# Attention probabilities transposed on VectorE in 32x32 blocks, and head sums and the sample's attention on small TensorE tiles

## The reference

```python
q, k, v, b_gate, c_gate, h, g_attn, g_conv = split(rmsnorm(x) @ w_in)
q, k = rope(rmsnorm_per_head(q)), rope(rmsnorm_per_head(k))
# prompt: chunk c sees chunks c-2, c-1 and c; sample: 128 cached keys and its own 32
s = (q @ k.T) * SCALE                      # masked to NEG_INF outside the window
m = max(max(s), sink)
p = exp(s - m) / (sum(exp(s - m)) + exp(sink - m))
attn = p @ v
u = c_gate * h;  conv_y = conv3(u)
merged = sigmoid(g_attn) * (attn @ w_attn_proj) + sigmoid(g_conv) * ((b_gate * conv_y) @ w_conv_proj)
x = x + merged @ w_out
y = x + (silu(xn @ w_ffn_gate) * (xn @ w_ffn_up)) @ w_ffn_down      # xn = rmsnorm(x)
```

## Time and profile before

| | us |
|---|---|
| median of 3 runs | 1734.26 |
| lowest and highest | 1733.05, 1735.46 |
| the profiled execution, its own time | 1733.39 |
| its span in the trace | 1731.6 |

### The profile page before, as it was taken

How to read it: one execution, slowest core, us unless ns; L and a number is a source line. 1 busy time by engine, 2 the same in 40 slices (tenths; PEclk the granted TensorE clock), 3 DMA queues, 4 the chain that set the end, 5 groups by cost and what they waited for, 6 DMA issues and landing times.

```text
span 1731.6 us, 35651 instructions
## 1 busy us (share of the span) xinstructions
PE 1714.1 (99%) x13944; PEld 1699.0 (98%) x13944; DVE 1014.1 (59%) x1268; ACT 809.4 (47%) x985; POOL 31.5 (2%) x54
## 2 busy tenths in 40 slices
PE   8899999999999999999999999999999999999999
PEld 7899999999999999999999999999999999999999
DVE  7876776767754444555565655554455554455565
ACT  6445655455554444434444555543344443334443
POOL 0100000000000000000000000000000000000000
PEclk9899999999999999999999999999999999999999
DMA  7455455555566566556566555565556556556555
GB/s 241 152 159 158 145 157 158 162 153 158 157 213 185 178 181 179 176 175 186 160 194 193 164 177 182 170 192 175 179 171 186 176 175 187 175 177 183 174 176 153
DMA packets 298626, 302.73 MB, mean 175 GB/s; under 512 B 9488, under 2 KB 296336, under 8 KB 298464
## 3 DMA queue, kind: packets, MB, share of 16 engines
q1 hardware_dynamic: 296544, 296.00, 56.4%
q0 software_dynamic: 752, 3.80, 0.6%
q10 hardware_dynamic: 1296, 2.46, 0.5%
HBM read 299.50 MB, written 2.72 MB: 175 GB/s over the span
## 4 chain that ended last, share of the span: by engine, by line
PE 97%; DVE 1%; DMA 1%; issue 0%; ACT 0%; SPq 0%; DVEq 0%; ACTq 0%
PE acc L1007 31%; PE acc L1009 31%; PE acc L1008 31%; DMA raw<-in_w_in 1%; PE side L1104 1%; PE side L1128 0%; PE side L1116 0%; PE side L1092 0%; DVE w_lo L595 0%; DMA region_x<-in_x_t 0%; PE side L1106 0%; DVE region_m L661 0%; PE side L1118 0%; PE side L1131 0%; ACT w_hi L373 0%
## 5 line engine op out<-in xcount | busy, mean ns | idle before, releaser
L595 DVE TENSOR_TENSOR w_lo<-raw,w_hi 128x1024 fp32r<-128x1024 f32 x567 | 688.6, 1225 | 537.0 <-ACT w_hi L373 528.8
L373 ACT ACTIVATE w_hi<-raw 128x1024 fp32r<-128x1024 f32 x567 | 593.2, 1054 | 612.9 <-PE acc L1009 608.4
L1007 PE MATMUL acc<-xn_hi,w_hi 128*128 128x288 f32 x2976 | 855.2, 287 | 1.1 <-DVE w_lo L595 1.1
L1008 PE MATMUL acc<-xn_lo,w_hi 128*128 128x288 f32 x2976 | 851.9, 286 | 0.0
L1009 PE MATMUL acc<-xn_hi,w_lo 128*128 128x288 f32 x2976 | 851.9, 286 | 0.0
L1007 PEld LDWEIGHTS acc<-xn_hi,w_hi 128*128 128x128 f32 x2976 | 563.3, 189 | 2.5 <-issue 1.5
L1008 PEld LDWEIGHTS acc<-xn_lo,w_hi 128*128 128x128 f32 x2976 | 563.3, 189 | 0.1
L1009 PEld LDWEIGHTS acc<-xn_hi,w_lo 128*128 128x128 f32 x2976 | 563.2, 189 | 0.0
L1007 PE MATMUL acc<-at_hi,w_hi 128*128 128x288 f32 x1216 | 347.9, 286 | 0.5 <-DVE w_lo L595 0.5
L1008 PE MATMUL acc<-at_lo,w_hi 128*128 128x288 f32 x1216 | 347.8, 286 | 0.0
L1009 PE MATMUL acc<-at_hi,w_lo 128*128 128x288 f32 x1216 | 347.8, 286 | 0.0
(11 more groups left out here) (180 smaller groups left out, 755.1 us busy)
## 6 DMA issues: line engine op xcount, KB each, us to landing
raw<-in_w_in SPq DMA_DIRECT2D x199, 512.0 KB, 4.4
raw<-in_w_ffn_gate SPq DMA_DIRECT2D x88, 512.0 KB, 4.5
raw<-in_w_ffn_up SPq DMA_DIRECT2D x88, 512.0 KB, 4.4
raw<-in_w_ffn_down SPq DMA_DIRECT2D x64, 512.0 KB, 3.7
raw<-in_w_attn_proj SPq DMA_DIRECT2D x32, 512.0 KB, 4.5
raw<-in_w_conv_proj SPq DMA_DIRECT2D x32, 512.0 KB, 4.4
raw<-in_w_out SPq DMA_DIRECT2D x32, 512.0 KB, 4.6
raw<-in_w_ffn_down SPq DMA_DIRECT2D x32, 384.0 KB, 3.7
```

The lines of the kernel that those rows point to most:

```text
L373: nc.scalar.activation(w_hi[:, s], raw[:, s], ACT.Copy).then_inc(S["hi_ready"], 1)
L595: V.tensor_tensor(w_lo[:, s], raw[:, s], w_hi[:, s].bitcast(F32), ALU.subtract).then_inc(S["lo_ready"], 1)
L1007: te.matmul(out, w_hi[:, s, k, cols], hi_b, start=first, stop=False)
L1008: te.matmul(out, w_hi[:, s, k, cols], lo_b, start=False, stop=False)
```

## The change

- VectorE transposes the probabilities with its own 32x32 block transposition (`STREAM_TRANSPOSE`, L758 and L834 of the changed kernel) from `probs` straight to their places in a new SBUF tile `probs_t`. There are sixteen of them per round over a 32-partition strip each; blocks that the mask makes zero in all heads are left out (`probs_t` is zeroed once at the start). They run in three parts, `turn_probs(0)` to `turn_probs(2)`, between the pieces of group g+3. The fourteen transposes on TensorE and the four copies on ScalarE are gone, and with them the semaphores `probs_normed`, `probs_in_psum` and `probs_copied`; `heads_out` waits for `probs_turned` and `values_staged`.
- The sums of squares are made by 64x64 tiles, one for each half of the rows and of the frames: 16 + 4 products in place of 4 + 1. The scores of the sample are two 64-row products in place of one of 128 rows, and its exponential, maximum and normalization are done in two halves of 64 partitions. `stats` has ten columns in place of nine.
- The sample's probabilities are transposed within 32x32 blocks by one instruction, and its output is made of 20 products of 32 rows, 64 columns and 32 frames each, in place of 4. Its values are laid out for that by 20 small copies on GpSimd, once in two rounds.
- VectorE does piece (g+3, 3) and (g+4, 0) ahead of the convolution taps in place of behind them; ScalarE does `at_hi` ahead of `z_hi`.

```diff
+            by_block = [a.rearrange("p u (m k) -> p u m k", m=3) for a in (probs, probs_t[:])]
+            def turn_probs(part):
+                for q in range(4):
+                    for r in range(4):
+                        middle_only, no_middle = q < 2 and r > 1, q > 1 and r < 2
+                        groups = slice(1, 2) if middle_only else slice(0, 3, 2) if no_middle else slice(0, 3)
+                        if (q * 4 + r) % 3 != part:
+                            continue
+                        of, to = (t[32 * p:32 * p + 32, :, groups, 32 * k:32 * k + 32]
+                                  for t, p, k in ((by_block[0], q, r), (by_block[1], r, q)))
+                        last = V.transpose(to, of)
+                if part == 2:
+                    last.then_inc(S["probs_turned"], 1)
...
-                V.tensor_scalar(probs_sample, probs_sample, s_inv[:, 8:9], None, ALU.mult
-                                ).then_inc(S["probs_normed"], 1)
+                for half in range(2):
+                    r = slice(64 * half, 64 * half + 64)
+                    own.mark(V.tensor_scalar(probs_sample[r], probs_sample[r], of_sample(s_inv, half), None, ALU.mult))
+                own.settle()
+                own.mark(V.transpose(probs_t_sample, probs_sample))
+                turn_probs(0)
                 ahead(g + 3, 1)
+                turn_probs(1)
                 ahead(g + 3, 2)
...
+                ahead(g + 3, 3)
+                turn_probs(2)
+                ahead(g + 4, 0)
                 for w in range(3):
...
-                ahead(g + 3, 3)
-
-                ahead(g + 4, 0)
                 ahead(g + 4, 1)
                 ahead(g + 4, 2)
...
             def head_sums(j):
-                pe.wait_ge(S["q_squared"], j + 2)
-                each_head = same_head.rearrange("p (h c) -> p h c", h=2)[:, :, 0]
+                wait_apart(pe, S["q_squared"], j + 2)
                 for n in range(2):
                     for t in range(2):
-                        c = 4 * n + 2 * t
-                        te.matmul(head_ssq[:, c:c + 2], head_b[:, t, n * HALF:n * HALF + P], each_head, start=True,
-                                  stop=True)
-                te.matmul(head_ssq[:, 8:9], squares_sample[:].rearrange("p h t n -> p (h t n)"), ones[:, 0:1],
-                          start=True, stop=True)
+                        for part in halves:
+                            for half, r in enumerate(halves):
+                                at = n * HALF + part.start
+                                te.matmul(head_ssq[part, half, 2 * n + t:2 * n + t + 1], head_b[r, t, at:at + 64],
+                                          ones[r, 0:1], start=True, stop=True)
+                for part in halves:
+                    for half, r in enumerate(halves):
+                        te.matmul(head_ssq[part, half, 4:5], squares_sample[r].rearrange("p t n -> p (t n)"),
+                                  ones[r, 0:1], start=True, stop=True)
...
-                for half, r in enumerate(rows):
-                    te.matmul(side[r, 1, 0:2 * TS], values_cur[:, 2], probs_t_sample[:, 0, r], start=True, stop=False)
-                for half, r in enumerate(rows):
-                    last = te.matmul(side[r, 1, 0:2 * TS], values_cur[0:TS, 3], probs_t_sample[0:TS, 1, r], start=False,
-                                     stop=True)
+                for kb in range(SAMPLE_BLOCKS):
+                    for q in range(4):
+                        half, t = q // 2, q % 2
+                        rows = slice(QUARTER * q, QUARTER * q + QUARTER)
+                        last = te.matmul(out_sample_t[halves[half], t], values_sample[rows, kb],
+                                         probs_t_sample[rows, kb * QUARTER:(kb + 1) * QUARTER], start=kb == 0,
+                                         stop=kb == SAMPLE_BLOCKS - 1)
```

More of the change, by code:

```diff
@@ L443, in _ @@
                 nc.scalar.activation(prompt(head_b), sums(0, slice(0, TP)), ACT.Square)
-                for half in range(2):
-                    r = slice(64 * half, 64 * half + 64)
-                    last = nc.scalar.activation(split(squares_sample[r, half]), sums(0, slice(TP, T))[r], ACT.Square)
-                last.then_inc(S["q_squared"], 1)
+                nc.scalar.activation(split(squares_sample), sums(0, slice(TP, T)), ACT.Square).then_inc(S["q_squared"], 1)
                 ahead(g + 2, 0)
@@ L744, in _ @@
                 own.settle()
-                for half in range(2):
-                    r = slice(64 * half, 64 * half + 64)
-                    last = V.tensor_copy(split(q_sample[r, half]), sample(head_a[r]))
-                last.then_inc(S["q_roped"], 1)
+                V.tensor_copy(split(q_sample), sample(head_a)).then_inc(S["q_roped"], 1)
                 dve.wait_ge(S["q_squared"], j + 2)
@@ L762, in _ @@
                             scalar=lowest, op0=ALU.add, op1=ALU.max, accum_out=s_max[:, c:c + 1]))
-                own.mark(V.reduce_max(s_max[:, 8:9], scores_sample, AX_X))
+                for half in range(2):
+                    own.mark(V.reduce_max(of_sample(s_max, half), scores_sample(half), AX_X))
                 dve.wait_ge(S["head_rms_ready"], j + 1)
@@ new lines, in all_scores @@
+                last.then_inc(S["scores_ready"], 1)
+            def heads_out(j):
+                pe.wait_ge(S["values_staged"], j + 1)
+                pe.wait_ge(S["probs_turned"], j + 1)
+                of_heads = probs_t[:].rearrange("p (t r) k -> p r t k", t=2)
+                for half, r in enumerate(halves):
+                    te.matmul(side[r, 0, :], values_cur[:, 0], of_heads[:, half, :, 0:2 * P], start=True, stop=False)
+                for half, r in enumerate(halves):
+                    te.matmul(out_t[r, :, P:2 * P], values_cur[:, 1], of_heads[:, half, :, 2 * P:3 * P], start=False,
+                              stop=True)
+                for kb in range(SAMPLE_BLOCKS):
+                    for q in range(4):
+                        half, t = q // 2, q % 2
[3 more added lines that the diff above has]
+                                         stop=kb == SAMPLE_BLOCKS - 1)
@@ L1150, in mix @@
                     if s == 1:
[L1152 removed]
+                        wait_apart(pe, S["side_free"], j + 1)
                         head_sums(j)
```

137 lines of the change are left out of this document (67 added, 70 removed).

## The result

The changed kernel takes 1744.54 us (median; 1744.13 to 1745.09), the kernel before, run beside it, 1733.92 us: 1.0062 times as long, 95% interval 1.005 to 1.0075, so 10.6 us more. I had predicted 1748, within 1729 to 1763, and slower with a chance of 0.72. Sign and size hold, but by luck: of the four terms only the first is right, the second has the wrong sign, the third is three times what it was, and the fourth, the one that decides, is a third of what it was. The errors cancel.

The account below looks back on a forecast made before the run. TensorE, busy 99% of the span, was taken to bound the kernel. Terms of -1.54 + 0.75 + 1.7 + 0.85 gave +1.76 us a round, +14.1 in 8 rounds: 1748 us median, range 1729 to 1763.

Parts of the forecast that it names:

- Term 1: The transposes on TensorE go, which takes 1.54 us a round off its path.
- Term 2: Head sums on TensorE by small tiles, 40 passes in place of ten: +0.75 us a round.
- the feed of 0.065 us a pass: Rate at which TensorE can be fed small passes, a load with its matmul: 40 passes take 2.6 us.
- rival A: Small passes on TensorE are fed fast enough and the change gains: -0.74 us a round, 1728 us; chance 0.17.
- Term 3: The sample's output on TensorE by small tiles, 20 products in 40 passes: +1.7 us a round.
- turn of the loop: Register work and branch behind the round's last pass on TensorE, no longer covered by lined-up passes: 0.5 us.
- Term 4: VectorE, with transpositions and other work added, comes late to piece (g+3, 1) and TensorE waits: +0.85 us a round.
- slack of 2.4 us: Time before the change between VectorE's `w_lo` for piece (g+3, 1), ready at 303.2, and TensorE beginning it at 305.63.
- The margin at (g, 3): Piece (g, 3), wanted 8.8 us into the next round, is ready at about 7 thanks to term 3's longer tail.
- Rival B: Transposing float32 on VectorE costs double: +5.1 us a round, 1775 us; chance 0.09.
- Rival C: Everything added is hidden and TensorE's losses equal its gains, feed about 0.04 us a pass: 1734 us; chance 0.12.
- the worse ends of terms 2 and 3: Upper ends for head sums, +1.7, and the sample's output, +2.8; together the round's sum was put at about +3.3 us.

Follow-up runs that it names:

- e9_no_turns_4of20: e1_no_turns with only 4 of the 20 small products of the sample's output (result wrong); 1719.04 us, 0.9916 of the kernel before.
- e11_sample_first: e10_rotated with the sample's 20 small products ahead of the four large ones at the end of the round; 1723.20 us, 0.9939 of the kernel before.
- e1_no_turns: The changed kernel without VectorE's sixteen transpositions of the prompt's probabilities (result wrong; the sample's stays); 1724.34 us, 0.9943 of the kernel before.
- e10_rotated: The changed kernel with VectorE's work reordered, ScalarE's first four exponentials one piece earlier, and piece (g, 3) prepared in the round before; 1724.49 us.
- e4_sample_4of20: The changed kernel with only 4 of the 20 small products of the sample's output (result wrong); 1743.97 us, 1.0055 of the kernel before.
- e5_exps_sooner: The changed kernel with VectorE's work reordered, ScalarE's first four exponentials ahead of piece (g+2, 2), and (g+2, 3) behind the last exponential; 1733.04 us.

## Why the prediction was right, and where not

- **Term 1, the transposes leave TensorE, -1.54 us a round: held** as far as it can be seen. TensorE's own round fell by 1.14; the other changes of its stream are read from rows, -0.41 (head sums), +0.15 (the sample's scores, 0.27 to 0.42) and +0.57 (`heads_out`, 1.81 to 2.38), which leaves -1.45 for the transposes.
- **Term 2, head sums, forecast +0.75, measured -0.41.** The step that failed is the feed of 0.065 us a pass, taken from a start after a wait. Those two rows are starts of an empty engine; the long row gives 0.015 us a pass. The scores start 0.69 us behind the head sums, by my own check a sign for rival A. The lower of my two prices, 0.055 us for a step of four tiles side by side, gave a gain of 0.3 and was nearly right. The Trainium skill, page "TensorE: Matmul & The Clock Gate", gives in section "Wait — 56ns, not 53.3ns?" about 62 ns per matmul with hardware decode off; at the 15 ns a pass measured here, that price is not the one paid. The same page of the Trainium skill, section "Part 3: Packing small matmuls — row/col tiling", has matmuls in different tiles start about 4 ns apart; the 15 ns agree with it in that small passes overlap, not in the figure.
- **Term 3, the sample's output, forecast +1.7, measured +0.57.** Same step, same cause; e9_no_turns_4of20 measures 32 of the 40 passes on their own, 0.69 us with the uncovered turn of the loop. The sentence on the turn of the loop was right in kind, since it is uncovered now, but it is 0.16 us and not 0.5. e11_sample_first covers it again.
- **Term 4, VectorE late, forecast +0.85, measured 2.54** (54.97 less 52.43). The place, the mechanism and the slack of 2.4 us were right. The size was wrong in three pieces. The first transpositions with the sample's take 2.92 us (308.11 to 311.03) and not 2.2, because each has about 0.18 us beyond its elements (2.66 us for six of 1536 elements at 1.02 ns) and not 0.07. The second exponential costs 0.68 (303.85 to 305.00 are 1.15 for two, where one took 0.47), not 0.47, the second half of the normalization 0.45 with its waits (2.86 in place of 2.41), not 0.31. Together 4.05 in place of 3.0, against a slack of 2.4 and the 0.15 by which the sample's longer scores hold TensorE back: 1.5, near the 1.45 of idle time. Then the second part, 3.77 us from piece step to piece step, for which I had 3.17, adds 0.83 and not 0.15, and a wait costs more than its idle time.
- **The margin at (g, 3)**, which I called gone "if term 3 does not cost anything", was gone. I read it as a margin of one place; it was the second ring, as long as the first to 0.2 us.
- **Rival A** was nearer on TensorE (-1.59 against the -1.14 measured, where I had +0.91), and where term 4 is away the time went below its 1728 (e1_no_turns and e10_rotated, 1724). **Rival B** falls: 384 elements take 564 ns, and an element 1.02 ns, no more than the 1.04 of the one-source rows. The Trainium skill, page "Vector Engine (DVE) Microarchitecture Reference", section "3.8 The reshape front-end and per-opcode configuration", gives one element per cycle per lane, and this trace agrees in that no second cycle shows. The sixteen waits are 16.0 us, between my 5 to 7 and B's 20. **Rival C** falls too: the feed costs less than it had, the waits more.

So the forecast of 1748 was near 1744.5 by luck: terms 2 and 3 were 2.3 us a round too dear and term 4 1.7 too cheap. One sum is off too: the worse ends of terms 2 and 3 together give -1.54 + 1.7 + 2.8 + 0.85 = +3.8 and not +3.3. The largest error was to treat the terms as a sum. They are not: with a ring setting the round, a change of TensorE's own work counts only as far as it lies in every ring of that length (e4_sample_4of20, outside ring 2: 0.7 us a round taken away, 0.1 gained). The head sums lie in both rings, so their 0.41 should have counted; no run takes them out.

What stays open: whether GpSimd's copies or the wider order of at and z cost anything by themselves (e1_no_turns bounds them near zero), and whether fewer, longer transpositions would do; neither was tried apart.

## What to carry to other kernels

When work goes to an engine with room on average, don't ask only which wait comes next: follow the chain from a point of the round around to the same point of the next, over every engine, and add it up for each way through; the longest ring is the time, and with a second ring just under it, shortening the first alone gives next to nothing. Price work in such a kernel by taking it out of two versions, one bound by the engine and one by the ring (here 5.3 and 0.6 us for the same edit). The rate at which an engine does many small instructions is read from a long row of them, never from its first starts after a wait; and idle time ahead of an answer from another engine is the place to put work, as e5_exps_sooner shows by taking work out of it.

## What the runs showed of the hardware

- Small float32 passes in four tiles go through TensorE at 15 ns each (32 in 0.49 us), eight for one of the 128x288 passes (0.1225 us).
- A wait costs TensorE 0.27 us more than the idle time in the view (3.77 - 2.94 = 0.83 for 0.56): 0.10 for a slower first step (0.22 us in place of 0.12), 0.17 from the modelled end of the matmul ahead of it.
- A block transposition on VectorE has a fixed part of some 0.18 us even back to back (six in 2.66 us, five in 2.51), so that 32 partitions by 128 elements, 304 ns, are more than half the price of three times as many, 564.
- ScalarE's exponential over 64 partitions takes what it takes over 128: 0.47 and 0.48 us for 160 columns, against 0.48. Up to the next instruction the two halves take 1.15 us (303.85 to 305.00), the one of before 0.47, so here splitting by partitions more than doubled it.
